# Both halves of the activations side by side in one matmul, and the merge stage with tokens stationary

## What is computed

```
first_block:
  h = h + hybrid_mixer(rmsnorm(h))     # delta rule, sliding window and stick-breaking branches, then
      merged = gate[:, :, 0] * (y_dn @ w_br_dn) + gate[:, :, 1] * (y_swa @ w_br_swa) + gate[:, :, 2] * (y_sb @ w_br_sb)
      return merged @ w_o              # gate = sigmoid(xn @ w_in[:, gates])
  h = h + memory_cross_attention(...)
  h = h + conv_ffn(rmsnorm(h)):        up = causal_dwconv(hn @ w_up, ffn_conv)   # 3 taps, 2048 -> 2 x 4096
                                       (silu(gate) * val) @ w_down
second_block (one layer, the conv mixer):
  mod = silu(c) @ mod_w + mod_b        # 2048 -> 12288: shifts, scales, gates
  u = a * sigmoid(gt);  u = 31-tap causal depthwise conv(u) + dw_b;  silu(layer_norm(u)) @ w_out
  u = square(relu(h @ mlp_w1));  x = x + (1 + g2) * (u @ mlp_w2)                 # 2048 -> 8192 -> 2048
```

## Time and profile before

| | us |
|---|---|
| median of 3 runs | 2741.73 (2739.86 to 2742.96) |
| the profiled execution | 2741.88 |
| its span | 2740.3 |
| TensorE busy | 2648.0 (97%) |
| DVE busy | 1835.2 (67%) |
| ACT busy | 1275.7 (47%) |
| POOL busy | 201.9 (7%) |
| DMA | 553.15 MB, mean 202 GB/s |

### The profile page before, as it was taken

One profiled execution on the slowest core, in us unless ns is written; L12 is line 12 of the kernel. 1 busy time (PEld: TensorE's weight loads), 2 busy tenths in 40 slices (PEclk: granted clock), 3 DMA queues, 4 the chain that ended last, 5 costly groups with the idle time before them and its releaser, 6 DMA issues.

```text
span 2740.3 us, 47131 instructions
## 1 busy us (share of the span) xinstructions
PE 2648.0 (97%) x18312; PEld 2466.9 (90%) x18312; DVE 1835.2 (67%) x2016; ACT 1275.7 (47%) x1629; POOL 201.9 (7%) x249
## 2 busy tenths in 40 slices
PE   7999999999999998999999989997989999999998
PEld 6999998999998887998899879896889898898997
DVE  5675647778778877776577656997665555555554
ACT  6544426533344445554344455665454334343342
POOL 1000000000000000000000002652000000000000
PEclk9999999999999999999999999998999999999999
DMA  5633435888989875776677644442555666666654
GB/s 185 177 116 101 131 96 194 304 288 307 328 305 328 286 257 191 263 240 222 191 260 241 222 139 154 148 153 70 184 155 185 193 184 189 190 181 192 188 184 153
DMA packets 269376, 553.15 MB, mean 202 GB/s; under 512 B 17025, under 2 KB 54962, under 8 KB 267954
## 3 DMA queue, kind: packets, MB, share of 16 engines
q1 hardware_dynamic: 249698, 442.06, 50.4%
q0 software_dynamic: 18720, 102.77, 11.2%
q10 hardware_dynamic: 816, 6.29, 0.6%
HBM read 548.96 MB, written 2.10 MB: 201 GB/s over the span
## 4 chain that ended last, share of the span: by engine, by line
PE 79%; DVE 8%; DMA 6%; ACT 3%; issue 2%; SPq 1%; POOLq 0%; DVEq 0%; ACTq 0%
PE sums L623 71%; DMA mod_raw<-in_mod_w_dram 3%; PE small L1493 3%; DVE w_lo L579 3%; DVE small L1676 2%; DVE mod_acc L1183 1%; ACT w_hi L570 1%; DMA raw<-in_conv_w_in_dram 1%; DMA raw<-in_w_br_dn_dram 1%; PE small L1616 1%; PE small L1195 1%; SPq L637 1%; DMA raw<-in_w_in_dram 1%; PE sums L1229 0%; DMA raw<-in_w_br_sb_dram 0%
## 5 line engine op out<-in xcount | busy, mean ns | idle before, releaser
L579 DVE TENSOR_TENSOR w_lo<-raw,w_hi 128x1024 fp32r<-128x1024 f32 x822 | 1012.5, 1240 | 742.1 <-ACT w_hi L570 739.2
L570 ACT ACTIVATE w_hi<-raw 128x1024 fp32r<-128x1024 f32 x822 | 868.3, 1059 | 1287.3 <-PE sums L623 1154.9
L623 PE MATMUL sums<-x_hi,w_hi 128*128 128x256 f32 x3984 | 1142.2, 287 | 13.8 <-DVE w_lo L579 8.3
L623 PE MATMUL sums<-x_lo,w_hi 128*128 128x256 f32 x3984 | 1131.3, 284 | 0.0
L623 PE MATMUL sums<-x_hi,w_lo 128*128 128x256 f32 x3984 | 1130.9, 284 | 0.0
L623 PEld LDWEIGHTS sums<-x_hi,w_hi 128*128 128x128 f32 x3984 | 768.6, 193 | 22.8 <-DVE w_lo L579 12.3
L623 PEld LDWEIGHTS sums<-x_lo,w_hi 128*128 128x128 f32 x3984 | 769.0, 193 | 1.4 <-issue 1.0
L623 PEld LDWEIGHTS sums<-x_hi,w_lo 128*128 128x128 f32 x3984 | 768.6, 193 | 0.0
L623 PE MATMUL sums<-w_hi,y_hi 128*128 128x512 f32 x928 | 364.9, 393 | 6.6 <-issue 6.4
L623 PE MATMUL sums<-w_hi,y_lo 128*128 128x512 f32 x928 | 363.4, 392 | 0.0
L623 PE MATMUL sums<-w_lo,y_hi 128*128 128x512 f32 x928 | 363.3, 392 | 0.0
(11 more groups left out here) (358 smaller groups left out, 2103.9 us busy)
## 6 DMA issues: line engine op xcount, KB each, us to landing
raw<-in_mlp_w_dram SPq DMA_DIRECT2D x256, 512.0 KB, 4.2
raw<-in_w_in_dram SPq DMA_DIRECT2D x198, 512.0 KB, 4.5
mod_raw<-in_mod_w_dram POOLq DMA_DIRECT2D x128, 768.0 KB, 6.4
raw<-in_w_up_dram SPq DMA_DIRECT2D x128, 512.0 KB, 4.3
raw<-in_w_down_dram SPq DMA_DIRECT2D x64, 512.0 KB, 4.5
raw<-in_conv_w_in_dram SPq DMA_DIRECT2D x128, 256.0 KB, 3.8
raw<-in_w_o_dram SPq DMA_DIRECT2D x32, 512.0 KB, 5.8
raw<-in_conv_w_out_dram SPq DMA_DIRECT2D x32, 512.0 KB, 4.0
```

The costliest lines, as they stand in the source:

```text
L570: act.activation(w_hi[:, s.slot(k), :], raw[:, s.slot(k), :], ACT.Copy).then_inc(hi_ready, 1)
L579: dve.tensor_tensor(w_lo[:, s.slot(k), :], raw[:, s.slot(k), :], w_hi[:, s.slot(k), :].bitcast(F32), ALU.subtract).then_inc(lo_ready, 1)
L623: mm = pe.matmul(o, l, r, start=first and i == 0, stop=end and i + 1 == len(steps), skip_group_check=True)
```

## The change

Five edits, together.

1. `x_hi` and `x_lo` lie side by side in `x_two`. The up chunks of the FFN and the MLP use `multiply_two`: per K tile and block one matmul of w_hi by both (512 columns, one bank) and one of w_lo by `x_hi` (256, onto the first half). A chunk takes four banks: m = 0 all of `sums`, m = 1 all of `small`. The two halves of each bank are added afterwards: ACT copies the second half to SBUF, DVE adds the first. In the FFN the newest tap is then taken by ACT from `pad2`, after that addition (`newest_tap`). In the MLP the Relu joins the square on DVE. Down chunks use banks of the same two sets (`down_sums`), and the FFN's mod sums go to a bank of `sums`.
2. The merge chunks have turned=False. The merged sum of a round is turned by 8 transposes in the first chunk of the next round (`turn_merged`; the last one in `mix_out`), copied by ACT (`keep_merged`), split by DVE (`split_merged`).
3. At the end of merge, down and cross_out chunks DVE works on the result one unit earlier.
4. Convolution: POOL adds 13 taps instead of 11, DVE does 18 instead of 20. In the last chunk TensorE does 11 per block instead of 19, POOL 8 instead of none, DVE 12 as before. The joins are one instruction for both blocks.
5. Loops over the MLP's down chunks are written out.

The diff, cut:

```diff
-POOL_TAPS = 11
-PE_TAPS_LAST = 19
+POOL_TAPS = 13
+POOL_TAPS_LAST = 8
+PE_TAPS_LAST = 11
...
-        x_hi = sb("x_hi", [P, KT, T], F32R)
-        x_lo = sb("x_lo", [P, KT, T], F32R)
+        x_two = sb("x_two", [P, KT, 2, T], F32R)
+        x_hi, x_lo = x_two[:, :, 0, :], x_two[:, :, 1, :]
...
+        def multiply_two(pe, s, bank, before=None):
+
+            pe.wait_ge(bank_read[s.pair], s.reads())
+            to = four(bank)
+            for k in range(s.size):
+                if before is not None:
+                    before(k * UK, (k + 1) * UK)
+                pe.wait_ge(lo_ready, s.rounds(k + 1))
+                for t in range(UK):
+                    kt = k * UK + t
+                    both = x_two[:, kt, :, :].rearrange("p a t -> p (a t)")
+                    for b in range(CH // P):
+                        c = slice(t * CH + b * P, t * CH + (b + 1) * P)
+                        pe.matmul(to[:, b, :], w_hi[:, s.slot(k), c], both, start=kt == 0, stop=False,
+                                  skip_group_check=True)
+                        mm = pe.matmul(to[:, b, 0:T], w_lo[:, s.slot(k), c], x_two[:, kt, 0, :], start=False,
+                                       stop=kt == KT - 1, skip_group_check=True)
+                mm.then_inc(unit_used, 1)
...
+            o = cv[:, CV_B * c:CV_B * (c + 1), :]
+            dve.tensor_tensor(o, dve_sums(c).rearrange("p (b t) -> p b t", t=T), o, ALU.add).then_inc(cv_added, CV_B)
...
+        def taps_join_last(dve, own):
+
             dve.wait_ge(cv_tap, TAPS_ONE * LAST + CV_B * DVE_TAPS_LAST)
+            dve.wait_ge(cv_pooled, POOL_TAPS * LAST + POOL_TAPS_LAST)
+            o = cv[:, CV_B * LAST:, :]
+            own.step(dve.tensor_tensor(o, dve_sums(LAST).rearrange("p (b t) -> p b t", t=T), o, ALU.add))
+            own.wait()
             dve.wait_ge(cv_diag_used, CV_B * PE_TAPS_LAST)
...
-            for c in range(CV_C - 1):
+            for c in range(CV_C):
                 pooled(pool, c)
...
+            def keep_merged(c, n):
+
+                act.wait_ge(merge_turned, n)
+                act.activation(m_hi[:, c, :], turned_merged, ACT.Copy).then_inc(merge_hi, 1)
...
-                    round_units(act, s, *ahead(s), beside)
+                    round_units(act, s, SLOTS, SLOTS + 3, beside)
+                    if m == 0 and not isinstance(i, int):
+                        keep_merged(bass.ds(i * 4 - 4, 4), at(0, (i, 1)))
+                    round_units(act, s, SLOTS + 3, s.size + SLOTS, beside)
...
-            def last_tap(s, to, f, i, m):
-
+            def newest_tap(s, to, f, i, m):
+
+                act.activation(pad2[:, :, FF_TAPS - 1:], cross_half(m), ACT.Copy).then_inc(ff_cross, 1)
+                act.wait_ge(bank_read[s.pair], s.reads(1))
                 for b in range(4):
                     w = parm_at("ffn_conv", at(2 * FF // P * (FF_TAPS - 1) + FF // P * m + b, (f, KT), (i, 4)))
-                    act.activation(to[:, b, :], chunk_sums(s)[:, b, :], ACT.Copy, scale=w)
+                    ins = act.activation(to[:, b, :], pad2[:, b, FF_TAPS - 1:], ACT.Copy, scale=w)
+                ins.then_inc(ff_newest, 1)
...
-                        act.activation(ml_r[:, :, :], chunk_sums(s), ACT.Relu).then_inc(bank_read[s.pair], 1)
+                        act.activation(ml_r[:, :, :], cross_half(m), ACT.Copy).then_inc(ml_cross, 1)
...
+            def split_merged(c, n):
+
+                dve.wait_ge(merge_hi, n)
+                dve.tensor_tensor(m_lo[:, c, :], turned_merged, m_hi[:, c, :].bitcast(F32), ALU.subtract).then_inc(merged, 1)
...
+                    end = s.size + SLOTS - (1 if m >= 3 else 0)
+                    rest_units(dve, s, SLOTS, end,
+                               first_chunk if m == 0 else lambda j: mod_unit(dve, kt + j, kt + j, (i, KT)), units, beside)
...
-                own.step(dve.tensor_copy(m_hi[:, c, :], gate[:, 0, :, :]))
-                own.wait()
-                dve.tensor_tensor(m_lo[:, c, :], gate[:, 0, :, :], m_hi[:, c, :].bitcast(F32),
-                                  ALU.subtract).then_inc(merged, 1)
+                    rest_units(dve, s, end, end + 1)
...
+                dve.wait_ge(ff_cross, at(m + 1, (f, 8), (i, 2)))
+                dve.tensor_tensor(pad2[:, :, FF_TAPS - 1:], main_half(m), pad2[:, :, FF_TAPS - 1:],
+                                  ALU.add).then_inc(bank_read[s.pair], 1)
                 dve.wait_ge(bank_read[s.pair], s.reads(1))
+                dve.wait_ge(ff_newest, at(m + 1, (f, 8), (i, 2)))
...
+                        dve.wait_ge(ml_cross, at(m + 1, (L[0], 4), (i, 2)))
+                        dve.tensor_tensor(ml_r[:, :, :], main_half(m), ml_r[:, :, :], ALU.add).then_inc(bank_read[s.pair], 1)
                         dve.wait_ge(bank_read[s.pair], s.reads(1))
-                        own.step(dve.tensor_tensor(ml_r[:, :, :], ml_r[:, :, :], ml_r[:, :, :], ALU.mult))
+                        own.step(dve.scalar_tensor_tensor(out=ml_r[:, :, :], in0=ml_r[:, :, :], scalar=0.0,
+                                                          in1=ml_r[:, :, :], op0=ALU.max, op1=ALU.mult))
...
+            def turn_merged(i):
+
+                pe.wait_ge(merge_sum, i + 1)
+                for b in range(4):
+                    for t in range(TT):
+                        ins = pe.transpose(small[:, b // 2, (b % 2) * T + t * P:(b % 2) * T + (t + 1) * P],
+                                           gates[:, 0, t, b * P:(b + 1) * P], ident[:, :])
+                ins.then_inc(merge_turned, 1)
...
-                    multiply(pe, spot("merge", m, L), x_hi, x_lo, True, beside=beside)
+                    multiply(pe, spot("merge", m, L), x_hi, x_lo, False,
+                             before=merge_before(i - 1) if i and m == 0 else None, beside=beside)
...
-                    multiply(pe, spot("merge", m, L), y_hi, y_lo, True, k0=k0)
+                    multiply(pe, spot("merge", m, L), y_hi, y_lo, False, k0=k0)
```

More of the change, by code:

```diff
@@ L2030, in _ @@
                     finished(s)
[L2031 to L2032 removed]
+                    newest_tap(s, ff_v, f, i, 1)
                 for c in range(4):
@@ L2233, in _, with between @@
                 s = spot("mix_out", c % 2, (c // 2, 16, 2))
-                rest_units(dve, s, *ahead(s), lambda j: mod_unit(dve, 4 * KT + kt + j, kt + j), units, beside)
+                def between(j):
+                    mod_unit(dve, 4 * KT + kt + j, kt + j)
+                    if c == 0 and j == 1:
+                        split_merged(slice(12, 16), 4)
+                rest_units(dve, s, *ahead(s), between, units, beside)
                 add_sums(s, c * CH)
@@ L2440, in _ @@
                 up(L)
-                with dve.Fori(0, 2) as i:
+                for i in range(2):
                     down(L, i, False)
@@ L2495, in _ @@
                 multiply(pe, spot("mix_out", c % 2, (c // 2, 16, 2)), m_hi, m_lo, False,
-                         before=None if c else lambda tile, end: pe.wait_ge(merged, tile // 4 + 1), beside=beside)
+                         before=None if c else merge_before(3, True), beside=beside)
             beside.rest()
```

155 lines of the change are left out of this document (96 added, 59 removed).

## The result

The changed kernel takes 2724.88 us in the median of 9 runs (2718.1 to 2732.9), the kernel before 2742.96 (2737.0 to 2746.9): ratio 0.9938, 95% interval 0.9928 to 0.9949. It is faster by 18 us where I forecast 45.

What follows compares the result with a forecast made beforehand. TensorE was taken to bound MLP and FFN up stages, TensorE and DMAs the merge, with DVE busy in the convolution. Savings of 13.8 + 11.4 + 8 + 1.5 + 7 + 3.5 = 45.2 from 2741.9 gave 2696.7 us, range 2680 to 2715.

Steps and rivals of the forecast that it cites:

- rival D: Up stages: a 512 followed by a 256 takes as long as three matmuls; 2724 us, chance 0.06 shared with another rival.
- The pair of matmuls, MLP 13.8 us: MLP up stage: three 256-column matmuls become one 512 and one 256, 13.5 ns saved each of 1024 times, 13.8 us.
- if mixing the lengths costs nothing: Up stages: assumption that a 512 and a 256 in alternation take 0.2265 + 0.1200 = 0.3465 us.
- FFN 11.4 us: FFN up stages: 13.8 us from joined matmuls less 2.4 us of stalls in the eight m = 0 chunks.
- Rival C: FFN: the handshake of ACT and DVE costs 1 us in each of 16 chunks; 2711 us, chance 0.09.
- Merge 8 us: Merge: 2 us saved in each of four rounds, about half of what TensorE wants; bounds 0 and 17.
- TensorE's 4.3 a round: Merge: saving per round if TensorE ruled, 5.2 us from wider matmuls against 0.87 us for eight added transposes.
- TensorE and the DMAs are at balance: Merge rounds: 95.6 and 95.8 us apart against 94.7 of TensorE's own time, so balanced within 1.1 us.
- reordering: Ends of merge, down and cross_out chunks: banks freed one unit earlier, 1.5 us gained, bounds 0 and 4.
- Convolution chunks 7 us: Convolution: moving taps from DVE to POOL saves net 1.06 us a chunk over some 6.5 chunks; bounds 3 and 10.
- two more additions cover one more `w_lo`, 0.5 us back: Convolution chunks: POOL's extra additions lengthen one more `w_lo` on DVE, 0.5 us against 1.56 us of taps saved.
- End of the convolution 3.5 us: Last convolution chunk: fewer TensorE taps, POOL's eight become last, 16.2 us instead of 19.5; 3.5 us, bounds 2 and 5.

Runs made afterwards that it cites:

- e4: Changed kernel with both matmuls of an up-chunk pair 512 columns wide (w_lo by both sisters too): 2935.74 us, measured once.
- e2: Changed kernel with up-chunk matmuls grouped by length, per K tile four of 512 columns, then four of 256: 2722.76 us, ratio to before 0.9922.
- e3: Changed kernel with up-chunk matmuls grouped over a unit of two K tiles, eight of 512 columns, then eight of 256: 2726.26 us, ratio to before 0.9935.
- e1: Changed kernel with the up chunks' pair of matmuls made three of 256 columns again: 2749.74 us, ratio to before 1.0029.
- e9: The changed kernel measured once more, nothing edited: 2732.36 us, ratio to before 0.9952.
- e7: Changed kernel with the merge and the first mix_out chunk as in the kernel before: 2736.63 us, ratio to before 0.9977.
- e5: Changed kernel with each modulation weight load cut from 1536 to 128 columns: 2703.05 us, measured once.
- e6: Kernel before the change with each modulation weight load cut from 1536 to 128 columns: 2732.01 us, measured once.
- e11: Changed kernel with the last two modulation units of a merge round moved behind the first gate product on DVE: 2720.35 us, ratio to before 0.9913.

## Why the prediction was wrong

The sign was right, the size was not: 45 us forecast, 18 measured (20.8 in the profiles), below the range's least gain of 27. No single rival came true: the time lies on D's 2724, but by coincidence, for D's pair of 0.36 did not come. Several terms were too large at once, and I had let the lower bounds of independent terms be "corners".

- **The pair of matmuls, MLP 13.8 us: measured 6.8.** The step that failed is "if mixing the lengths costs nothing". The pair takes 0.3533 us where the two pace rows add to 0.3465; half the saving goes (1024 x 6.8 ns = 7.0 us). That lies halfway to rival D. e4 shows that one length alone keeps 0.2265, e2 and e3 that fewer changes of length bring part of it back. I took two rows from uniform streams for a stream that alternates, and weighed the gap as all or nothing. The hidden part was right: e1 shows that copy, add and square cost the MLP nothing.
- **FFN 11.4 us: measured 3.5, and about 1 without the clock.** The two stages went from 376.4 to 372.9 us. Before, both do the same work in 189.5 and 186.9 us, and the 2.6 between them is the clock, which was still at half when the first began and is at full in the changed kernel's:

```profile
1072.20:1077.90 5.70, 5.70 (x27) 5.70 (x28) 5.70 (x10) 2.94 (x5) 0.00 (x0) 0.50 0.01 3
```

  That part of the gain is luck. With the pair at 0.3533 (16 units at 2.77) the saving is 7.7; the waits for `w_lo` in the two stages take 4.2, and a stall costs more than its wait: two units around one take 3.43 and 2.93 us where two others take 5.66, 0.70 for a wait of 0.44, some 2 us more over eight. The step that failed, beside the pair, is the size of the stalls: I had 2.4 for them, in the right place, eight stalls four units behind an m = 0 chunk, but 0.43 to 0.65 us of wait each where I said 0.3. Rival C's 1 us in every chunk did not come. Left out was that with the new handshake a late load of raw weights reaches TensorE: 0.4 us here, 5.9 in one stage of e9, 1.2 to 2.8 at a time in e1, e2, e3 and e7.
- **Merge 8 us: measured 1.4 over three rounds, and 1.7 ahead of them.** TensorE's 4.3 a round was nearly right (4.2 in e5 and e6, 3.9 over all traces). The step that failed is "TensorE and the DMAs are at balance": with e11's order the same loads fit a round of 90.7. The changed order left one `w_lo` fewer between the last two modulation units, the second of which stands in front of the gate product that frees the bank, and TensorE waited 3.2, 1.1 and 1.1 us for it. So the **reordering**, which I had at +1.5, took this away; in the two down stages it gave 2.8. At the end of cross_out TensorE's last chunk ends 2.1 us sooner, and then the modulation sum waits 3.8 us for DVE's last modulation unit, a wait that the trace of before does not have: nothing is won there. The rest is the clock: 0.96, 0.98 and 0.98 in rounds that before had 1.00, some 1.5 us for each 0.02. So 12.9 (three rounds at 4.3) less 5.4 of waits and 6 of clock leaves about the 1.4. That the trace of before had no fall in its three rounds is chance: e6 has two, e7 three.
- **Convolution chunks 7 us: measured -1.8 (4.6 of the stage less 6.4 at its end).** The step that failed is "two more additions cover one more `w_lo`, 0.5 us back". Of six `w_lo` four got longer, by 0.3 to 1.0 us, 2.1 in all against 1.6 of taps removed. The Trainium skill (SBUF — State Buffer, "SBUF: two separate sides") states that the shared port pair is an exclusive lock for a whole instruction. From that I had worked out that the edit could bring nothing, had set it aside, and it brought nothing. The trace agrees with the direction and not with the rule in full: no `w_lo` lost a whole addition of 1.7 us (the most was 1.0, from 1.21 to 2.19). Whether the lock is the cause, no run here shows.
- **End of the convolution 3.5 us: measured 6.4.** From the last GLU to the first conv_out matmul it is 22.4 us instead of 28.8. POOL's eight additions took 11.17 us, 1.40 each, where I had 1.71; no `w_lo` ran beside them:

```profile
1872.65 11.17 POOL L1708 TENSOR_TENSOR cv<-cv,cv_p 128x512 f32<-128x512 f32 x8 [6.13 <-ACT cv_p L1692]
...
1871.68 12.01 PE L1665 MATMUL small<-pad,tap_diag 128*128 128x256 f32 x44 [8.48 <-DVE pad L2423]
...
1883.92 0.69 DVE L1742 TENSOR_TENSOR cv<-small,cv 128x512 f32<-128x512 f32 x1 [2.65 <-POOL cv L1708]
```

TensorE's 44 took 12.0, within my 10.8 to 13, and POOL released the join, as forecast, though only 0.1 us behind TensorE's end.

The chain of the sum: 45.2 less 7.0 (MLP pair), 7.9 (FFN), 3.6 (merge and reordering: 9.5 forecast, and 1.7 + 1.4 + 0.1 + 2.8 less 0.1 in the stages' table), 8.8 (chunks), plus 2.9 (end) gives 20.8, the difference of the two spans. Still open is why wide matmuls start later behind narrow ones, why the clock falls behind one modulation sum and not behind another, and what the changed merge is worth in the median, where e7 says 4 to 12 us.

## What to carry to other kernels

Price a merged instruction from a stream with the same mix, not from two uniform ones; here the mix left half of the saving. Before comparing a stage of two traces, take out of both what the clock cost: it gave the FFN 2.6 us and took some 6 from the merge. Before reading a high DMA share as the bound, look at what stands in front of the instruction that frees TensorE's bank: moving two operations that wait for a load behind it gave some 7 us in three rounds without one byte less. And a tap moved from DVE to POOL is paid back in every `w_lo` that then runs beside POOL: count those. DVE's own taps keep their length (477 ns with 13 additions on POOL, 478 with 11).
